# A two-block transformer kernel on one core: the shared key/value stage and the last output block in another sequence

## The reference, cut to what matters

```
h = x
h = h + (silu(gate) * groupnorm(retention(q, k, v))) @ ret_w_out            # retention layer
h = h + sigmoid(rmsnorm(h) @ ple_w_gate[0]) * (p[0] @ ple_w_emb[0])         # "ple0", "emb0"
kc, vc, ks, vs, kw, vw = split(rmsnorm(h, kv_norm) @ kv_w)                  # shared keys/values, 4 groups x 128
k_cmp, v_cmp = compress(kc), compress(vc)    # blocks of 32 tokens, stride 16: W1 (4096x256), gelu, W2
q, gate, bgate = split(rmsnorm(h, nsa_norm) @ nsa_w_in)
h = h + (silu(gate) * attention(q, k_cmp, v_cmp, ks, vs, kw, vw, bgate)) @ nsa_w_out
h = h + sigmoid(rmsnorm(h) @ ple_w_gate[1]) * (p[1] @ ple_w_emb[1])
x = rmsnorm(h, final_norm)
# second block
u, v, z, q, k, vh, zb, ga, gb = split(x @ w_in)
merged = sigmoid(ga) * (branch_a(u, v, z) @ wa) + sigmoid(gb) * (diff_attention(q, k, vh, zb) @ wb)
y = alpha * x + merged @ w_out + sigmoid(x @ w_ple_gate) * (p_2 @ w_ple)
out = (y - mean(y)) * rsqrt(var(y) + eps) * ln_g + ln_b                     # rows of 1024
```

## Time and profile before

| | us |
|---|---|
| median of 3 runs | 887.86 (887.0 to 888.1) |
| the profiled execution | 886.9 |
| its span in the profile | 885.1 |
| TensorE (PE) busy | 865.4 (98%) |
| VectorE (DVE) busy | 580.5 (66%) |
| ScalarE (ACT) busy | 492.9 (56%) |
| GpSimd (POOL) busy | 37.7 (4%) |

### The profile page before, as it was taken

How to read it: one execution, slowest core, us unless ns; L and a number is a source line. 1 busy time by engine, 2 the same in 40 slices (tenths; PEclk the granted TensorE clock), 3 DMA queues, 4 the chain that set the end, 5 groups by cost and what they waited for, 6 DMA issues and landing times.

```text
span 885.1 us, 12251 instructions
## 1 busy us (share of the span) xinstructions
PE 865.4 (98%) x4866; PEld 747.5 (84%) x4866; DVE 580.5 (66%) x908; ACT 492.9 (56%) x742; POOL 37.7 (4%) x49
## 2 busy tenths in 40 slices
PE   9999999999999999899999999999999999999995
PEld 8998888888799889899898788888888887888884
DVE  5976666627677763567575556798458547667775
ACT  6434445436654854668578555755534438766630
POOL 0000000000200000000000001200020000000002
PEclk9999999999999999999999999999999999999998
DMA  8864644624557774442333445574754526455411
GB/s 312 280 212 166 190 146 144 199 96 167 191 191 259 253 259 160 173 122 90 123 118 122 143 167 183 204 250 159 275 194 163 172 94 230 151 190 191 143 48 47
DMA packets 81479, 154.34 MB, mean 174 GB/s; under 512 B 3792, under 2 KB 12112, under 8 KB 81424
## 3 DMA queue, kind: packets, MB, share of 16 engines
q1 hardware_dynamic: 79920, 149.17, 49.6%
q0 software_dynamic: 1360, 4.33, 1.7%
q10 hardware_dynamic: 144, 0.07, 0.0%
HBM read 152.51 MB, written 1.05 MB: 173 GB/s over the span
## 4 chain that ended last, share of the span: by engine, by line
PE 92%; DVE 3%; ACT 2%; issue 1%; DMA 1%; POOL 1%; POOLq 0%; SPq 0%; DVEq 0%; ACTq 0%
PE acc L2048 11%; PE acc L2050 10%; PE acc L2049 10%; PE acc L2031 9%; PE acc L2033 9%; PE acc L2032 9%; PE acc L2057 7%; PE acc L2059 7%; PE acc L2058 7%; PE misc L2209 2%; PE misc L2077 2%; DVE wlo L1367 1%; PE misc L2198 1%; ACT whi L917 1%; PE misc L2248 1%
## 5 line engine op out<-in xcount | busy, mean ns | idle before, releaser
L1367 DVE TENSOR_TENSOR wlo<-raw,whi 128x2048 fp32r<-128x2048 f32 (+2 forms) x146 | 317.0, 2189 | 88.3 <-ACT whi L917 87.4
L917 ACT ACTIVATE whi<-raw 128x2048 fp32r<-128x2048 f32 (+2 forms) x146 | 267.2, 1837 | 146.9 <-PE acc L2050 71.4
L2048 PE MATMUL acc<-whi,xhiA 128*128 128x512 f32 x272 | 108.0, 397 | 0.0
L2049 PE MATMUL acc<-wlo,xhiA 128*128 128x512 f32 x272 | 106.0, 390 | 0.0
L2050 PE MATMUL acc<-whi,xloA 128*128 128x512 f32 x272 | 106.0, 390 | 0.0
L2031 PE MATMUL acc<-whi,xhiA 128*128 128x512 f32 x240 | 93.8, 391 | 0.0
L2033 PE MATMUL acc<-whi,xloA 128*128 128x512 f32 x240 | 93.5, 389 | 0.0
L2032 PE MATMUL acc<-wlo,xhiA 128*128 128x512 f32 x240 | 93.4, 389 | 0.0
L2057 PE MATMUL acc<-xhiC,whi 128*128 128x256 f32 x256 | 73.7, 288 | 3.7 <-issue 3.7
L2059 PE MATMUL acc<-xhiC,wlo 128*128 128x256 f32 x256 | 73.2, 286 | 0.0
L2058 PE MATMUL acc<-xloC,whi 128*128 128x256 f32 x256 | 73.1, 286 | 0.0
(11 more groups left out here) (298 smaller groups left out, 1720.1 us busy)
## 6 DMA issues: line engine op xcount, KB each, us to landing
raw<-in_w_in_dram SPq DMA_DIRECT2D x36, 1024.0 KB, 5.3
raw<-in_ret_w_in_dram SPq DMA_DIRECT2D x22, 1024.0 KB, 5.2
raw<-in_nsa_w_in_dram SPq DMA_DIRECT2D x16, 1024.0 KB, 5.3
raw<-in_kv_w_dram SPq DMA_DIRECT2D x12, 1024.0 KB, 5.8
raw<-in_ret_w_out_dram SPq DMA_DIRECT2D x8, 1024.0 KB, 5.0
raw<-in_ple_w_gate_dram SPq DMA_DIRECT2D x8, 1024.0 KB, 5.7
raw<-in_nsa_w_out_dram SPq DMA_DIRECT2D x8, 1024.0 KB, 5.1
raw<-in_cmp_w_k_dram SPq DMA_DIRECT2D x4, 1024.0 KB, 5.2
```

Source lines behind the costliest of these rows:

```text
L917: nc.scalar.activation(whi[plan.slot[c]][:, 0:size], raw_part(c), ACT.Copy).then_inc(hi_done, 1)
L1367: nc.vector.tensor_tensor(wlo[plan.slot[c]][:, 0:size], raw_part(c), whi[plan.slot[c]][:, 0:size].bitcast(F32), ALU.subtract).then_inc(lo_ ...
L2048: nc.tensor.matmul(o, xh, hi[:, j, off:off + cols], start=start, stop=False)
L2049: nc.tensor.matmul(o, xh, lo[:, j, off:off + cols], start=False, stop=False)
```

## The change

It does six things.

1. `emb0`, `emb1`, `emb2` (the weights of p) are loaded as one chunk 1024 wide each rather than two of 512: 143 chunks in place of 146.
2. The key/value stage begins with vs rather than kc, and takes its two chunks by token tile: chunk 0 for the rows of tile 0, chunk 1 for tile 0, then both for tile 1. The transposes of tile 0 come between `emb1_0` and `emb1_1`, those of tile 1 after vs for tile 0's first chunk. The square sum of tile 0 moves ahead of the last sigmoid, and its normed rows ahead of the last residual addition. The operand is split by 128x128 pieces (`rows_hi`, `rows_lo`).
3. The fourth slot is lent from `ks[1]` instead of `kc[0]`, and the copies of the keys are merged: four on ACT and five on DVE for each of ks and kw.
4. The order afterwards: `cmp_k[1]` and `[2]` together between `ks[1]` and `kw[0]`, `cmp_k[3]` between kw's chunks, `cmp_v` between the chunks of vw and `nsa_q0`, `nsa_g0[0]` ahead of `nsa_b`, `bgT` last.
5. DVE splits the first chunks of the next group before the scores of group 0 instead of after those of tile 0.
6. At the end the second chunks of `wo0` and `wo1` are taken by token tile: wo0 and wo1 for tile 0, then both for tile 1. DVE finishes the first half of tile 0's columns (`scaled_rows(0, 0)`) within tile 1's sums; ACT and POOL do the other half only.

```diff
     r("emb1_0")
+    norm("kv", (0, 1))
     r("emb1_1")
-
-    norm("kv")
+    plan.half("vs", 0, 0, True)
+    norm("kv", (2, 3))
+    plan.half("vs", 1, 0, True)
+    plan.half("vs", 0, 1, True)
+    plan.half("vs", 1, 1, True)
     r("kc")
     r("vc")
     r("ks", [0])
     r("cmp_k", [0])
     r("ks", [1])
-    r("cmp_k", [1])
+    r("cmp_k", [1, 2])
     r("kw", [0])
-    r("cmp_k", [2, 3])
+    r("cmp_k", [3])
     r("kw", [1])
-    r("vs", [0])
+    r("vw", [0])
     m("hidT", 0)
     r("cmp_v", [0])
-    r("vs", [1])
+    r("vw", [1])
     r("cmp_v", [1])
+    r("nsa_q0", [0])
+    r("cmp_v", [2])
+    r("nsa_q0", [1])
+    r("cmp_v", [3])
     m("kcmp")
-    r("vw", [0])
-    r("cmp_v", [2, 3])
-    r("vw", [1])
-    r("nsa_q0")
+    r("nsa_g0", [0])
     m("hidT", 1)
     r("nsa_b")
     m("vcmp")
+    r("nsa_g0", [1])
     m("bgT")
-    r("nsa_g0")
...
     r("wo1", [0])
-    r("wo0", [1])
-    r("wo1", [1])
+    for part in range(MT):
+        plan.half("wo0", 1, part)
+        plan.half("wo1", 1, part)
...
-    plan.slots(plan.chunk_no[("kc", 0)], plan.upto[("T", NG - 1, 1, HPG - 1)] + AHEAD)
+    plan.slots(plan.chunk_no[("ks", 1)], plan.upto[("T", NG - 1, 1, HPG - 1)] + AHEAD)
...
-                        for a in range(2):
-                            nc.scalar.activation(keysA[0][2 * b + a][:, at_:at_ + P], src[:, a, 0:P], ACT.Copy)
-                            ins = nc.scalar.activation(keysB[0][2 * b + a][:, at_:at_ + P], src[:, a, P:T], ACT.Copy)
+                        nc.scalar.activation(keysA7[:, 2 * b:2 * b + 2, at_:at_ + P], src[:, :, 0:P], ACT.Copy)
+                        ins = nc.scalar.activation(keysB8[:, 2 * b:2 * b + 2, at_:at_ + P], src[:, :, P:T], ACT.Copy)
...
+                split_until(plan.chunk_no[("vs", 1)] + 1)
+                asked = norm_stats("kv", 1)
+                rows_lo(0, "kv", "B")
+                norm_rows("kv", 1, asked)
+                rows_lo(1, "kv", "B")
+                split_until(plan.chunk_no[("kc", 0)] + 1)
+                for j in (2, 3):
+                    rows_lo(j, "kv", "B")
...
                 dve.wait_ge(stack_zero, 2)
+                split_until(plan.chunk_no[group_fill(0)[1]] + 1)
                 for g in range(NG):
...
+                split_until(len(plan.chunks))
+                for m in range(MT):
+                    for nb in range(2):
+                        name = f"wo{nb}"
                         tile_wait(dve, name, m)
                         piece = h[:, m, nb * HALF:nb * HALF + HALF]
                         freed[name] = link(nc.vector.tensor_tensor(piece, piece, pair(name)[m][:], ALU.add))
                         link(nc.vector.bn_stats(stat[:, nb, m], piece))
+                        if m and nb == 0:
+                            dve.wait_ge(*asked)
+                            dve.wait_ge(gain_in[0], 48)
+                            scaled_rows(0, 0)
```

More of the change, by code:

```diff
@@ L118, in block, with half @@
         self.blocks[name] = dict(chunks=chunks, orient=orient, xt=xt)
-    def half(self, name, i, part):
+    def half(self, name, i, part, rows=False):
         b = self.blocks[name]
@@ L224, in weight_blocks @@
         for i in range(2):
-            std(f"emb{n}_{i}", src, i * HALF, 2, "nat", "P", kper=2)
+            plan.block(f"emb{n}_{i}", [((f"emb{n}", 0), src.rearrange("(k p) n -> p k n", p=P), range(2), D,
+                                        i * HALF, HALF, i == 1)], "nat", "P")
     for i in range(2):
@@ L433, in xt_order @@
     o += [("norm", "ple0", j) for j in range(4)] + [("p", 1)]
-    o += [("norm", "kv", j) for j in range(4)] + [("cmp", "k"), ("norm", "nsa", 0), ("norm", "nsa", 1)]
+    o += [("rows", m, half) for m in range(MT) for half in range(2)] + [("cmp", "k"), ("norm", "nsa", 0), ("norm", "nsa", 1)]
     o += [("cmp", "v"), ("norm", "nsa", 2), ("norm", "nsa", 3)]
@@ L2004, in operand, with chunk @@
                 return xhi[s][:, k, m0:m1], xlo[s][:, k, m0:m1]
-            def chunk(name, i, first, last, part=None):
+            def chunk(name, i, first, last, part=None, rows=False):
                 blk = plan.blocks[name]
@@ L2020, in chunk @@
                 ins = None
-                if blk["orient"] == "nat" and last:
+                if blk["orient"] == "nat" and (last or rows):
                     for m in range(MT):
```

213 lines of the change are left out of this document (123 added, 90 removed).

## The result

| | before | after |
|---|---|---|
| median of 4 runs, us | 887.43 (886.83 to 888.1) | 875.66 (875.5 to 876.03) |
| the profiled execution | 886.9 | 875.75 |
| its span | 885.1 | 873.7 |
| PE busy | 865.4 | 862.9 |

The ratio is 0.9868 (95% interval 0.9853 to 0.9883): 11.8 us faster by the medians, 11.15 by the profiled executions, 11.4 by their spans. So direction and most of the size were right, and 2 us of gain were missed. PE's idle time fell from 19.7 to 10.8 us, and its busy time by 2.5.

The account below looks back on a forecast made before the run. PE bounds the kernel, busy 865.4 of 885.1 us. Terms -0.9 -1.4 -0.6 -0.6 -0.5 +0.7 -5.2 -1.7 = -10.2 took 886.9 to 876.7, plus 1.0 for the median gives 877.7; range 875.8 to 881.8.

Parts of the forecast that it names:

- A: Start of the key/value stage: most of PE's 1.34 us of waits for normed rows and xloB goes; gain 0.9 us.
- F: At nsa_g0: one new wait, for the accumulator pair cmp_v filled, freed by hidden("v") on ACT; cost 0.7 us.
- E: At bgT: the 0.5 us wait for nsa_b's sigmoid goes because nsa_g0[1] now lies between; gain 0.5 us.
- B: At kw behind ks: the 1.35 us wait on keys_lo is covered by cmp_k[1] and [2]; gain 1.4 us.
- H: Behind the last matmul: tile 0's results and POOL's power come earlier, L1989's halves run faster; gain 1.7 us.
- C: At kw[1]: the 0.56 us wait on a low part goes, its slot now coming from cmp_k[2]; gain 0.6 us.
- D: At vw: the 0.64 us wait on a low part goes, covered by alternating with cmp_v; gain 0.6 us.
- G: Group 0: DVE's earlier splits remove the 3.72 us stop at nsa_q1[0] and 1.5 us of low clock; gain 5.2 us.
- the first: Small waits stay or come at the alternating hand-overs, making 2 to 3.5 us: 879 to 882.5; chance 0.17.
- The second: Group 0's wait stays, not being DVE's or held by nsa_g0's accumulators; gives 5.2 back, about 883; chance 0.07.
- The third: Start wait wholly gone, nsa_g0's new wait hidden by kcmp, end gains 1.9: 875 to 876.3; chance 0.06.
- The fourth: New short stops make PE's clock fall for long between 236 and 365: 888 or more; chance 0.025.

Follow-up runs that it names:

- number 1: The kernel before with one line added: DVE splits nsa_q1's two chunks ahead of group 0's scores; 881.58 us, ratio 0.9938.
- number 3: The changed kernel without the early-split line and with DVE's split limits at vcmp and bgT set down; 880.96 us.
- 6: The changed kernel with all four key/value transposes together behind emb1_1 and ahead of vs; 881.42 us.
- 10: The kernel before with only the new end (wo0[1] and wo1[1] by token tile, scaled_rows(0, 0) on DVE); 886.51 us, ratio 0.9993.
- number 5: The changed kernel with the fourth slot lent from kc[0] rather than ks[1]; 878.12 us.
- number 7: The changed kernel with the four transposes together, but ACT's square and DVE's normed rows in the order of before; 878.95 us.
- number 4: The kernel before with cmp_k[1] and [2] together ahead of kw[0], slots dealt as before; 887.79 us, ratio 1.0014.
- 2: The changed kernel without the one line that splits nsa_q1 ahead of group 0's scores; 876.02 us.
- number 8: The changed kernel with bgT ahead of nsa_g0[1]; 875.93 us.
- number 11: The changed kernel without scaled_rows(0, 0) on DVE: ACT and POOL do both halves of tile 0 again; 874.7 us, ratio 0.986.
- 12: The changed kernel with both halves of tile 0 on ACT and POOL and hidden() as one copy instead of two; 874.26 us, ratio 0.9852.
- number 9: The changed kernel with cmp_v[3] ahead of nsa_q0[1], and hidden("v") ahead of the queries' copies on ACT; 876.01 us.

## Why the prediction was right in its direction and 2 us short

Two steps of the prediction failed: the last of its sum, "the median lies 1.0 over it (887.86), so 877.7", where 0.09 under the profiled execution was measured; and the terms A to F, which put a wait at its idle time alone and so had 3.3 us where 4.73 were measured. Without the added 1.0 the forecast would have been 876.7, and with the waits at their measured cost 876.3. The mechanisms of the terms were right but for E's cause and a condition that B left out, and H was sized too large. By the spans the gain is 11.4 where 10.2 was forecast: 1.43 more ahead of group 0, 0.13 more in it, 0.34 less at the end. Of the 1.2 more, 0.25 does not show in the time of the profiled execution, which has that much more over its span. So part of the sum's error is hidden by H and by these 0.25, which is luck.

**The last step of the sum.** I took 876.7 for the profiled execution (measured 875.75) and added 1.0 because the three runs of before had their median 1.0 above its profiled execution. That 1.0 belonged to the kernel before and not to the method: 35 further runs of it, beside the three sets of experiments, have their medians at 886.89 (21 runs), 886.86 (7) and 887.99 (7): twice on the profiled 886.9, once 1.1 above. And the changed kernel's median is 0.09 below its profiled run. What lifts some runs of before is most likely the clock behind the stop of 3.7 us: of the 21 runs the two with the longest spans (886.0 and 886.5) have a mean clock of 0.992, the two shortest (884.7 and 884.9) 0.995, and number 1, without the stop, has no such runs. Where the clock fell in them is not shown, since they were not profiled. Four kernels with a stop of about that length spread by 1.2 to 2.6 us (before, number 3, 6 and 10), the two with a stop of 1.6 to 2.0 in the changed kernel by 2.0 and 2.3 (5, 7), number 4, which has one of each, by 3.3. Those without one spread by 0.7 or less (after, 1, 2, 8, 11, 12), but for number 9 (one of its four runs, which have stops of 0.56 or less behind the first 60 us, lies 2.2 higher than the others, and why is open). The change removes the stop, so the forecast should have removed the offset with it.

**The price of a stop.** Terms A to F took the idle time that the wait shows. The profiles give more: one stop fewer at equal idle time is worth 0.3 (number 4), a stop of 1.64 costs 1.97 (number 5). The rows tell why at least half of it: matmuls of 256 columns start 0.12 apart when they follow one another, but each is shown as 0.28 long; the idle time begins at the shown end, so 0.16 of the lost time is booked as busy. The rest lies in the first matmul behind the stop, which is shown 0.35 to 0.39 long instead of 0.28; behind the stop at 282.25 the next one starts 0.22 later instead of 0.12. This price is an estimate from single profiles. The stretch up to the first scores came out 1.43 better than forecast. Of this 0.63 is idle time (4.40 in six waits fell to 0.47, 3.93 less, where I had 3.3: 0.45 kept at A and 0.7 for F were too much). The other 0.8 is the stops' price, 5 x 0.3 = 1.5, less some 0.6 that the steps between the halves of vs take longer now: emb1_1 3.09 and the first two halves 2.85 and 2.82, against 2.72 for the others.

Point by point, the cost in before less that in after by the starts of the PE steps:

| term | forecast | measured | |
|---|---|---|---|
| A start of the stage | 0.9 | 1.4 | no wait over 0.15 left; I kept 0.45 idle |
| B and C, kw | 2.0 | 2.4 | idle 1.91 gone, and two stops' price |
| D vw | 0.6 | 1.0 | the wait is gone; no run moved this alone |
| E bgT | 0.5 | 0.7 | gone, but not for the cause I gave (number 8) |
| F nsa_g0 | -0.7 | -0.8 | idle 0.47 and a stop's price |
| G group 0 | 5.2 | 5.3 | right; caused by either of two edits (1 to 3) |
| H end | 1.7 | 1.4 | the new L2019 cost 0.5 against before where I had 0.1 |

No run takes item 1 of the change (emb as one chunk) apart; the stretches that hold emb0 and emb2 are equal within 0.1 us, so it is worth little here. **A** was right in its mechanism (number 7); one reading was wrong, since the row of seven transposes was taken for all sixteen, which end at 241.25 and not at 240.3. The low part ahead of xloB ends at 241.36, so how much of the wait of 1.04 was the low part's stays open; the term counts the wait whichever it was. **B** was right that the accumulators' wait would be covered by 3.8 us of cmp_k, but silent on the second condition: with before's slots the same order gains nothing (4, 5). The text named the slot only for kw[1]. **F** is shown by numbers 9 and 12: it is the second of two copies, and the rows of the new wait are these (PE, and the first of ACT's copies):

```profile
337.11 0.39 PE L2114 MATMUL acc<-xhiC,whi 128*128 128x256 f32 x1 [0.47 <-ACT arena L1097]
```

```profile
336.29 0.38 ACT L1097 ACTIVATE arena<-acc 60x256 f32<-60x256 f32 x1 [0.41 <-PE acc L2128]
```

**H** went wrong at one term: "The new L2019 ... has 2.7 us for 0.7 + 0.7 + 0.7, or up to 1.3 for the last". It took 1.72 beside POOL's addition, and the list ahead of it was late itself: the centring of tile 0 (1.27) ends at 863.1, when the accumulators of the next half have been there for 0.4 us. The last addition starts 0.84 behind the end of the last matmul, in before 0.35 (875.80 against 875.45): 0.49 lost where I had 0.1. Against an addition that DVE's list doesn't hold up it is the 0.79 of number 11, which takes the operation away. From the last addition to the span's end it takes 7.45 instead of 9.30, 1.85 less where I had 1.8, so the other parts held: POOL's power directly behind its request, L2039 at 1.27, L2019's two halves at 1.41, where 1.4 was forecast. On this the Trainium skill, "GPSIMD Engine Reference", section 1 "Specifications", was the better guide: it has GpSimd and VectorE contend when the latter reads two inputs from SBUF. The trace agrees: 1.72 beside POOL's addition, 0.7 each for the last two halves. By that rule the forecast of the end was 1.4, the measured value; the prediction doesn't show how it came to these 0.3 less, and 1.72 is beyond its own bound of 1.3, so that the figures meet is partly luck.

**The rivals.** Of the first (small waits where the order alternates) nothing came: PE was busy through 282 to 325 while the loads rose from 252 to 267 GB/s. Its mechanism is real, though, one step away: numbers 4, 5 and 9 each reached it by moving one chunk or one slot. The second (the stop in group 0 isn't DVE's) is refuted by number 1. The third, more gain, with 0.06, has the measured time in its 875 to 876.3, but not for its reasons: of its three only the first came (the start wait gone), F kept 0.47 and the end gained 1.4 and not 1.9. It was given too little, because neither the small stops' price nor a missing offset was in its terms. The fourth (a lower clock) had no part in the result (mean clock 0.996 to 0.998), nor had the fifth.

On the clock the Trainium skill, "TensorE: Matmul & The Clock Gate", section "A second HAM failure mode: psum-queue depth-cycling", has frequent short idles make it fall and rise. It stood at 1.00 from 282 to 325 in before with three of them, and at 1.00 in number 1 from 236 to 360, with all six of 0.3 to 1.35 in it. No trace here shows the clock fall for short waits of that size.

## What to carry to other kernels

A stop of PE costs its shown idle time and, by an estimate from two pairs of profiles, about 0.3 us more in this kernel, so many small stops are worth more than the list of waits says; and when a long stop behind which the clock falls is removed, expect the offset between the typical run and the profiled one to go with it. A wait with the releaser "issue" can still be an engine's order: look at what stands ahead of the missing operand's instruction on the engine that makes it, and at every edit that moves it, since two can do the same. Before an operation is moved from POOL or ACT to an engine with "free" time in a tail, add up that engine's list from the last thing it waited for, with the longer durations that it shows beside POOL.

## What the runs showed of the hardware that I had not expected

Number 3, with a stop of 3.6 us, is longer than the changed kernel by 3.9 us in two runs and by 6.5 in two others, with mean clocks of 0.997 and 0.993: the loss behind a stop isn't a constant of the kernel. The two kernels with stops of 1.6 to 2.0 us each have runs that are 1.7 to 2.3 us longer than the profiled one; in number 7, whose profile shows the clock at 1.00 from 235 to 255, these have a mean clock of 0.995 instead of 0.997, in number 5 the mean clock is 0.996 in both. Whether the clock fell there behind that stop is not shown, since only one execution of each was profiled.

A DVE operation on 128x512 with both inputs in SBUF took 1.72 us beside a POOL addition and 0.7 alone. In number 11 an addition with one input from the accumulators and a row sum with a single input took 0.69 each beside POOL's additions (864.44 to 866.95), as long as without them.

A copy of 124 rows on ACT took 0.38 us, as did one of 60 rows with the same 256 columns.
